# A fourth bank for turned keys, score products three units behind, and new-token scores in the output bank

## The reference

```python
# layer 0, FoX: 8 heads of 64, past of 4096 rows in 32 pages of 128 per sequence, plus the 8 new rows
s = einsum('bqhd,bkhd->bhqk', q_i, k) * ATTN_SCALE + cum_q - cum_k     # causal
out = einsum('bhqk,bkhd->bqhd', softmax(s), v)
# layer 1, dilated: 16 heads of 64, window buffer of 2048 rows per sequence, plus the 8 new rows
for w, d in ((128, 1), (512, 4), (2048, 16)):   # keys at distances 0, d, 2d, ... up to w
    m, den, o = masked softmax statistics;      # mixed per position and head by den * exp(m)
```

## Time and profile before

| | |
|---|---|
| median of 3 runs | 2801.06 us (2792.39 to 2810.39) |
| the profiled execution's own time | 2801.74 us |
| its span in the trace | 2800.1 us |
| mean granted clock of TensorE | 0.881 of full speed |
| FoX past stage | 284 to about 712 us |
| dilated past stage | about 1978 to 2290 us |

### The profile page before, as it was taken

One profiled execution on the slowest core, in us unless ns is written; L12 is line 12 of the kernel. 1 busy time (PEld: TensorE's weight loads), 2 busy tenths in 40 slices (PEclk: granted clock), 3 DMA queues, 4 the chain that ended last, 5 costly groups with the idle time before them and its releaser, 6 DMA issues. The chain is left out here.

```text
span 2800.1 us, 65133 instructions
## 1 busy us (share of the span) xinstructions
PE 2309.0 (82%) x26373; PEld 1779.5 (64%) x26373; DVE 1434.0 (51%) x2248; ACT 873.0 (31%) x1576; POOL 378.8 (14%) x585
## 2 busy tenths in 40 slices
PE   7868788886877699679999979959677767899998
PEld 3544677774643587457777757734566645677776
DVE  2425677775244556674532352358566646554223
ACT  2324444442113122233322222117333323333222
POOL 1002133433000000001110000124111101111000
PEclk8888798987886799789999989989887778999999
DMA  7320899997346100213323322350799952233231
GB/s 236 106 65 3 264 357 319 369 325 268 99 161 221 47 4 3 56 44 91 90 76 90 90 67 83 99 200 18 215 288 272 286 162 58 64 89 90 84 90 56
DMA packets 308558, 392.24 MB, mean 140 GB/s; under 512 B 25616, under 2 KB 226650, under 8 KB 308308
## 3 DMA queue, kind: packets, MB, share of 16 engines
q1 hardware_dynamic: 275332, 277.96, 32.4%
q0 software_dynamic: 32976, 110.79, 12.1%
HBM read 377.98 MB, written 10.70 MB: 139 GB/s over the span
## 5 line engine op out<-in xcount | busy, mean ns | idle before, releaser
L801 PE MATMUL bank<-yT,WH 128*128 128x288 f16 x3200 | 532.4, 290 | 45.7 <-DVE yT L661 35.4
L854 DVE SCALAR_TENSOR_TENSOR WL<-wring,WH 128x1024 f16<-128x1024 f32 x194 | 255.6, 1322 | 290.6 <-ACT WH L834 290.6
L801 PEld LDWEIGHTS bank<-yT,WH 128*128 128x128 f16 x3200 | 316.3, 99 | 131.8 <-issue 39.2
L1294 DVE TENSOR_TENSOR KL<-bank,KH 128x512 f16<-128x512 f32 x416 | 283.6, 688 | 204.0 <-ACT KH L1270 195.4
L1189 PE MATMUL bank<-cst,kslot 128*128 128x128 f32 x1664 | 311.2, 318 | 77.9 <-DMA kslot<-in_cache_fox_k 39.9
L1270 ACT CAST KH<-bank 128x512 f16<-128x512 f32 x416 | 242.5, 584 | 398.7 <-PE bank L1189 398.7
L801 PE MATMUL bank<-uT,WH 128*128 128x288 f16 x2048 | 338.2, 288 | 11.0 <-DVE WL L854 11.0
L801 PE MATMUL bank<-yT,WL 128*128 128x288 f16 x1600 | 332.1, 290 | 0.0
L834 ACT ACTIVATE WH<-wring 128x1024 f16<-128x1024 f32 x194 | 203.4, 1053 | 308.1 <-PE bank L801 221.4
L1189 PEld LDWEIGHTS bank<-cst,kslot 128*128 128x128 f32 x1664 | 203.7, 158 | 106.1 <-DMA kslot<-in_cache_fox_k 47.1
L801 PEld LDWEIGHTS bank<-uT,WH 128*128 128x128 f16 x2048 | 201.7, 99 | 63.6 <-issue 11.6
(11 more groups left out here) (429 smaller groups left out, 3582.2 us busy)
## 6 DMA issues: line engine op xcount, KB each, us to landing
kslot<-in_cache_fox_k SPq DMA_DIRECT2D x256, 256.0 KB, 5.4
vslot<-in_cache_fox_v POOLq DMA_DIRECT2D x256, 256.0 KB, 5.5
wring<-in_ada_w SPq DMA_DIRECT2D x96, 512.0 KB, 4.9
kslot<-in_state_dil_k SPq DMA_DIRECT2D x80, 512.0 KB, 10.6
vslot<-in_state_dil_v POOLq DMA_DIRECT2D x80, 512.0 KB, 16.1
wring<-in_mlp_up SPq DMA_DIRECT2D x64, 512.0 KB, 4.1
wring<-in_mlp_down SPq DMA_DIRECT2D x64, 512.0 KB, 3.7
wring<-in_ev_w_in SPq DMA_DIRECT2D x26, 512.0 KB, 3.8
```

The source lines that it names most:

```text
L801: last = nc.tensor.matmul(bank[b + h][:, 0:HALF], w[s % 2][:, c, :], x[:, s % parts * KC + c, h * HALF:(h + 1) * HALF], start=(s % parts = ...
L854: nc.vector.scalar_tensor_tensor(WL[s % 2][:, :, :], w[:, :, :], WSCALE, WH[s % 2][:, :, :], ALU.mult, ALU.subtract).then_inc(w_free, 1)
L1294: nc.vector.tensor_tensor(KL[i][:, :], turned[n % NT][:, :], KH[i][:, :], ALU.subtract).then_inc(lo_out, 1)
```

## The change

The turned keys get a fourth bank, bank 4; KH and KL get a fifth buffer each; `LAG` is 3 instead of 2. `LEAD` goes up by one in both calls (FoX 2 to 3, dilated 0 to 1), so `values` keeps its distance to the products. The scores of the new tokens, which had bank 4, go to unused columns of the sequence's output bank, 160 to 223 (and 416 to 479 for the second set of 8 heads of the dilated stage). The wait for that bank moves from the first `values` to `new_scores`, and the add of the mask is done for each set of 8 heads.

```diff
-        NB = 4
-        LAG = 2
+        NB = 5
+        LAG = 3
         VLAG = nu + LEAD
-        turned = [bank[i] for i in (0, 1, 6)]
+        turned = [bank[i] for i in (0, 1, 6, 4)]
...
                     def new_scores(s):
-                        if s:
-                            pe.wait_ge(new_out, s)
+                        pe.wait_ge(clear, 2)
+                        if s >= 2:
+                            pe.wait_ge(o_out, (s - 1) * E)
                         for e in range(E):
                             for j in range(4):
-                                last = nc.tensor.matmul(bank[4][0:NDEC, 64 * e + 16 * j:64 * e + 16 * j + 16], KNEW[:, j + 4 * e, :],
+                                at = 256 * e + 160 + 16 * j
+                                last = nc.tensor.matmul(mixed[s % 2][0:NDEC, at:at + 16], KNEW[:, j + 4 * e, :],
                                                         QB[:, s * E + e, j, :], start=True, stop=True)
...
-                        if u0 == 0:
-                            if s >= 2:
-                                pe.wait_ge(o_out, (s - 1) * E)
-                            else:
-                                pe.wait_ge(clear, 2)
...
-                        nc.vector.tensor_tensor(new[0:NDEC, :].rearrange("p (h q) -> p h q", q=8), bank[4][0:NDEC, 0:W].rearrange("p (h q) -> p h q", q=8),
-                                                new_bias_of(s), ALU.add).then_inc(new_out, 1)
+                        for e in range(E):
+                            rows, at = new[0:NDEC, 64 * e:64 * e + 64], 256 * e + 160
+                            nc.vector.tensor_tensor(rows.rearrange("p (h q) -> p h q", q=8),
+                                                    mixed[s % 2][0:NDEC, at:at + 64].rearrange("p (h q) -> p h q", q=8),
+                                                    new_bias_of(s)[:, 8 * e:8 * e + 8, :], ALU.add).then_inc(new_out, 1)
...
-                        dve.wait_ge(new_out, s + 1)
+                        dve.wait_ge(new_out, (s + 1) * E)
...
-            attend_past(PAGES // 2, 1, 2, 4, 8, 2, 4, (QB, QH, QL), KNEW, VNEW, load_page("cache_fox_k"), load_page("cache_fox_v"), bias_of,
+            attend_past(PAGES // 2, 1, 2, 4, 8, 3, 4, (QB, QH, QL), KNEW, VNEW, load_page("cache_fox_k"), load_page("cache_fox_v"), bias_of,
...
-            attend_past(DILT, 2, 2, 4, 8, 0, 0, (QB, QH, QL), KNEW, VNEW, load_tile("state_dil_k"), load_tile("state_dil_v"),
+            attend_past(DILT, 2, 2, 4, 8, 1, 0, (QB, QH, QL), KNEW, VNEW, load_tile("state_dil_k"), load_tile("state_dil_v"),
```

## The result

The changed kernel took **2834.33 us** (median of 4 runs, 2824.07 to 2839.52), the kernel before 2803.36 us (4 runs, 2792.39 to 2810.39): ratio 1.011, 95% interval 1.0062 to 1.0157. The prediction said 2797 us, at most 2809. It was wrong in size and in sign. Timed again on another chip the changed kernel took 2825.16 us against 2803.99, ratio 1.0069 (1.0043 to 1.0094), so some 20 us are the kernel's. The two intervals overlap, and I take the other ten of the first result for spread.

What follows compares the result with a forecast made beforehand. DMA was taken to bound both stages, with VectorE setting the pace at FoX's boundaries. Terms -4.8 + 0.4 + 0 + 0.6 = -3.8 us from 2801.74 gave 2797.9, stated as 2797 us after the 0.7 lower median; range 2783 to 2809.

Steps and rivals of the forecast that it cites:

- What bounds the kernel: Both stages: dilated DMA share 0.99, almost none idle; FoX 0.93, 24 us idle, with VectorE setting the pace at boundaries.
- KL waits are 4.4 us and DMA is full: 0, with +0 and -2 as bounds: Dilated stage: the longer lag changes nothing, 0 us, at most 2 us faster and no slower.
- Fourth bank, LAG 3, -4.8 us in FoX: FoX boundaries: key slots come free earlier, so DMA moves 0.68 us earlier at 7 boundaries, -4.8 us; bounds 0 and 24.
- Fill, +0.4 us: Start of each stage: first values and first maxima come one iteration later, +0.3 us in FoX, +0.4 us together.
- New scores, +0.6 us: Dilated stage: one mask add becomes two on the path to the exponent, +0.6 us, bounds 0 and +1.2.
- Rival 3: Boundaries of both stages: keys a unit ahead crowd out values, slower, about 2811 us; chance 0.13.
- Rival 2: FoX boundaries: TensorE meets the keys' backlog at full pace and most holes fill, -20 us, about 2781; chance 0.12.
- 358 GB/s: FoX's middle: possible HBM ceiling, allowing only 17 us less; 387 GB/s in one window spoke for the higher figure.

Runs made afterwards that it cites:

- best_again: Kernel before with, in FoX only, fourth bank, fifth KH/KL, LAG 3, LEAD 2, all-reduce ahead of the seventh value tile; new scores in output bank: 2785.44 against 2809.31 us.
- banks_only: Kernel before with four banks, five KH/KL and new scores in the output bank, but old LAG 2 and old LEAD in both stages: ratio 0.9998.
- pairs: Changed kernel, but TensorE turns a key tile's second unit ahead of a value group that stood behind its first: 2805.36 against 2804.70 us for the kernel before.
- after_again: The changed kernel unaltered, timed once more on another chip: 2825.16 us against 2803.99 us for the kernel before, ratio 1.0069.

## Why the prediction was wrong

**What bounds the kernel**: right. Both stages are DMA's, and FoX's idle DMA time is what can be won: `best_again` takes 14 to 22 us less than unchanged FoX stages (419.6 to 428.4), within the 24 us that the prediction gave as its upper bound.

**"KL waits are 4.4 us and DMA is full: 0, with +0 and -2 as bounds"**: this step failed. The stage measured +14 to +19 us. I took a full DMA for a sign that nothing can be won there, which is right, and put the bound on the slower side at +0, which doesn't follow: with a DMA share of 0.99 and four slots, 25 us of DMA time went idle as soon as slots came free later. The sentence ahead of it holds the error: "every consumer [...] moves one unit later against turn". For values the first and the second unit of a tile aren't alike. One unit later carries every value group across the middle of a key tile, from behind its second unit to behind its first. That a slot is free when both units of its tile are turned stood in the description of the kernel, and the prediction used it for its FoX term, but asked only how much earlier a slot comes free, not what now stands between the two units. TensorE's order of instructions shows it without a run; the prediction read that order for the lag alone.

**Fourth bank, LAG 3, -4.8 us in FoX**: the signs were as said (waits for KL 35.9 to 8.9 us, waits for keys up; spacing of the all-reduces (671.60 - 379.73) / 6 = 48.6 us for 48.8, forecast 48.1), the size was not. Changed FoX stages took 421.5 to 426.7 us, unchanged ones 419.6 to 428.4: 0 within 4 us. The term left out what the values' place costs, in FoX too: with the second unit turned first the same lag gives 412.5 us. What the lag alone is worth depends on the rest: 8 to 9 us with the later all-reduce, none seen without it.

**Fill, +0.4 us**: too small to be seen in stages that spread by 9 us. **New scores, +0.6 us**: nothing that can be measured, by `banks_only`, whose interval is -0.3 to +0.2%, some 6 us each way.

**Rivals.** Rival 3 had the sign and not the cause: it had keys crowd out values, with waits for values above 30 us. They fell to none in 2038:2308 of the changed kernel and to 6.4 us in 2015:2310 of `after_again`. What happened is nearer to its opposite: key loads are issued late, DMA rests, and then values come in a burst ahead of the late keys. Its price, 10 us above the kernel before, was half of what came. Rival 2's condition (TensorE meets the backlog with a unit in hand) wasn't tested by the change; `pairs` took 9 to 14 us off the changed kernel's FoX stage. The 358 GB/s that I weighed as a ceiling do not bind here: by the Trainium skill ("DMA: Bandwidth & Descriptors", section Bandwidth) HBM grants a core some 358 GB/s when its pair streams too, and 425 was measured with the pair idle; `best_again` moved 365 GB/s for 232 us.

**Chances**: 0.03 for slower by over 1%, where the first result lay at 1.1% and the repeat at 0.7%. The condition that I named for it (more than twice rival 3) was of the wrong mechanism.

## What to carry to other kernels

Where a resource reads full, what can be gained is bounded by its idle share, but that share says nothing of what can be lost: ask of every shift what releases its slots. A shift by one step matters by what it crosses; if buffers are freed every second step, odd and even shifts are different changes, and a long group of work is better placed behind a release than ahead of it. When waits change their name and a stage keeps its length, look whether two effects cancel, by an experiment that moves one of them alone.

## What the runs showed of the hardware

- Key loads that are issued behind GpSimd's burst of value loads wait for it, although they are on another queue. GpSimd issues its burst from 2149.76 on in the changed kernel, and in 2153:2159 the values' queue (q0) has all of the DMA time, while loads of key tiles were issued at 2154.32 and 2156.83; later both share it evenly, as in 2161:2167, at 406 GB/s. The kernel before has the same behind its burst (q0 104.0% in 2125:2127, a key load issued at 2125.66). Queue, packets, MB, share of 16 engines:

```profile
q0 software_dynamic: 395, 1.43, 102.7%
...
q0 software_dynamic: 328, 1.21, 50.9%
q1 hardware_dynamic: 328, 1.21, 50.8%
```

- A full DMA (share 1.03 and 1.02) moves 238 GB/s in the first of these windows and 406 in the second. Bytes per second don't tell whether DMA is full in this stage; the share does. What makes the difference isn't shown.
- The code between the two stages, the same in all kernels, took 1264.1 to 1286.5 us in single executions, a spread as large as what the whole change costs; TensorE's granted clock in 1062:1114 was 0.63 to 0.95 in them.
